# Hymba-style encoder layer on one core: when the three lent weight pieces are issued

## The reference, cut to what matters

```python
def hier_moe(h, w_group, b_group, w_expert, b_expert, w_gate, w_up, w_down):
    ...
    # top-1 group of 4, then top-2 of its 8 experts: expert_idx (T, 2), gates (T, 2)
    flat_e = expert_idx.reshape(A)
    order = jnp.argsort(flat_e)
    ...
    xb = h_pad[buf_tok].reshape(n_blocks, MOE_BLOCK, D)
    def expert_block(args):
        x_b, e = args
        hid = jax.nn.silu(x_b @ w_gate[e]) * (x_b @ w_up[e])
        return hid @ w_down[e]
    ...
    y_assign = yb[dest_orig].reshape(T, TOP_K, D)
    return jnp.einsum('tkd,tk->td', y_assign, gates.astype(h.dtype))
```

## Time and profile before

| | |
|---|---|
| median of 3 runs | 865.64 us (865.56 to 866.73) |
| the profiled execution's own time | 866.06 us |
| its span, first to last instruction | 864.2 us |
| granted TensorE clock, mean | 0.994 |
| PE busy | 833.4 us (96%) |
| DVE, ACT, POOL busy | 414.7, 216.0, 139.9 us |
| moved by DMA | 261.94 MB, 303 GB/s over the span |
| DMA, GB/s in the 22 slices (21.6 us each) from 346 us on, without the last two | 317 to 422 |

### The profile page before, as it was taken

How to read it: one execution, slowest core, us unless ns; L and a number is a source line. 1 busy time by engine, 2 the same in 40 slices (tenths; PEclk the granted TensorE clock), 3 DMA queues, 4 the chain that set the end, 5 groups by cost and what they waited for, 6 DMA issues and landing times.

```text
span 864.2 us, 16000 instructions
## 1 busy us (share of the span) xinstructions
PE 833.4 (96%) x5930; PEld 566.9 (66%) x5931; DVE 414.7 (48%) x796; ACT 216.0 (25%) x461; POOL 139.9 (16%) x279
## 2 busy tenths in 40 slices
PE   7999999999999999899999999999999999999995
PEld 5888988777877887765555555555555555555541
DVE  4699999986565532753222222222222222222237
ACT  3423211457875333101111011110111101111013
POOL 3300010000000011112222212222112222122101
PEclk9999999999999999999999999999999999999999
DMA  7353544221254198899999999999999999999998
GB/s 198 79 137 101 185 178 177 59 87 35 76 168 127 69 414 333 317 363 407 418 418 418 375 411 419 414 420 419 419 419 419 422 419 420 420 419 422 419 385 318
DMA packets 81141, 261.94 MB, mean 303 GB/s; under 512 B 19273, under 2 KB 45129, under 8 KB 56522
## 3 DMA queue, kind: packets, MB, share of 16 engines
q1 hardware_dynamic: 63392, 240.92, 71.3%
q0 software_dynamic: 7888, 18.78, 5.6%
q10 hardware_dynamic: 9818, 1.66, 1.0%
HBM read 246.49 MB, written 24.20 MB: 313 GB/s over the span
## 4 chain that ended last, share of the span: by engine, by line
PE 81%; DVE 13%; DMA 2%; issue 2%; ACT 1%; SPq 1%; POOL 0%; POOLq 0%; DVEq 0%; ACTq 0%
PE ps L1468 29%; PE ps L1514 16%; PE ps L1203 9%; PE ps L1339 8%; DVE big L1945 7%; PE ps L1482 3%; PE ps L1408 3%; PE ps L1255 2%; PE ps L1222 2%; DMA big<-results 2%; PE ps L1234 1%; PE ps L1471 1%; PE ps L1162 1%; DVE w_split L1882 1%; DMA results<-big,to_of 1%
## 5 line engine op out<-in xcount | busy, mean ns | idle before, releaser
L1471 PE MATMUL ps<-ring,big 128*64 128x256 f32 x688 | 154.1, 382 | 0.6 <-DMA ring<-in_w_up 0.6
L1468 PE MATMUL ps<-ring,big 128*64 128x256 f32 x672 | 150.4, 382 | 1.6 <-issue 1.6
L1203 PE MATMUL ps<-hT,w_split 128*128 128x256 f32 (+1 forms) x744 | 136.9, 341 | 0.0
L1468 PEld LDWEIGHTS ps<-ring,big 128*64 128x64 f32 x672 | 92.6, 138 | 56.0 <-issue 12.5
L1203 PEld LDWEIGHTS ps<-hT,w_split 128*128 128x128 f32 x744 | 113.5, 190 | 20.5 <-issue 7.0
L1807 ACT ACTIVATE big<-ps 64x256 f32<-64x256 f32 x78 | 29.3, 376 | 389.4 <-PE ps L1471 346.9
L2234 DVE TENSOR_TENSOR big<-ps,big 64x256 f32<-64x256 f32 x78 | 33.2, 426 | 181.5 <-ACT big L1807 170.9
L1471 PE MATMUL ps<-big 128*64 128x256 f32 x544 | 120.2, 379 | 0.0
L1468 PE MATMUL ps<-big 128*64 128x256 f32 x544 | 120.2, 379 | 0.0
L1468 PEld LDWEIGHTS ps<-big 128*64 128x64 f32 x544 | 74.5, 137 | 46.5 <-issue 9.7
L1471 PEld LDWEIGHTS ps<-ring,big 128*64 128x64 f32 x688 | 94.7, 138 | 2.0 <-DMA ring<-in_w_up 1.0
(11 more groups left out here) (294 smaller groups left out, 1196.5 us busy)
## 6 DMA issues: line engine op xcount, KB each, us to landing
ring<-in_w_down SPq DMA_DIRECT2D x44, 1024.0 KB
ring<-in_w_up SPq DMA_DIRECT2D x43, 1024.0 KB, 14.5
ring<-in_w_gate SPq DMA_DIRECT2D x42, 1024.0 KB, 11.2
big<-in_w_gate SPq DMA_DIRECT2D x20, 1024.0 KB, 7.2
big<-in_w_up SPq DMA_DIRECT2D x20, 1024.0 KB
big<-in_w_down SPq DMA_DIRECT2D x20, 1024.0 KB
w_raw<-in_w_in SPq DMA_DIRECT2D x20, 512.0 KB, 3.9
results<-spare POOLq DMA_DIRECT2D x12, 512.0 KB, 3.2
```

Of the source, the lines that this page charges most:

```text
L1203: mm = pe.matmul(ps[:, n % 2, 0:size], w_split[:, sub, hi_w, k, :], hT[:, k // 4, hi_h, k % 4, cols], **flags)
L1468: pe.matmul(ps[0:BLK, 6 * h, 0:FH], xT[:, k, q, :], gate[2][:, k, fs], **flags)
L1471: mm = pe.matmul(ps[BLK:2 * BLK, 6 * h + 1, 0:FH], xT[:, k, q, :], up[2][:, k, fs], **flags)
```

## The change

Lent piece 0 now waits until `pool_passed` is 1, the other two until it is 2 (in place of the first gather's landing). POOL counts `pool_passed` up behind each of the first two gathers.

```diff
@@ -906,8 +906,9 @@
                 _, _, w, ks = pieces[0][b]
                 sp.dma_start(lent[:, b], weights_of(SLOTS, w, ks)).then_inc(lent_in[b // 2], 16)
 
+            sp.wait_ge(pool_passed, 1)
             load_lent(0)
-            sp.wait_ge(xb_in[0], 16)
+            sp.wait_ge(pool_passed, 2)
             load_lent(1)
             load_lent(2)
 
@@ -1087,6 +1088,7 @@
             for q in range(2):
                 pool.wait_ge(idx_ready, q + 1)
                 fetch(q)
+                pool.sem_inc(pool_passed, 1)
             pool.wait_ge(xb_copied, 1)
             pool.wait_ge(idx_ready, 3)
             fetch(0)
```

## The result

| | before | changed |
|---|---|---|
| median | 865.98 us | 869.84 us |
| lowest, highest of 12 | 864.79, 867.85 | 867.21, 870.75 |
| profiled execution, own time and span | 866.06, 864.2 us | 869.46, 867.6 us |

The ratio is 1.0042, with a 95% interval of 1.0035 to 1.0049: 3.0 to 4.2 us slower. The forecast was 867.8 us, with a range to 869.6. The direction was right; the time lies 0.2 us outside the range. Disturbed executions (three of the kernel before at 1001 to 1195 us, two of after_dve at 885 and 950 us) are left out of every median and ratio of this document.

The account below looks back on a forecast made before the run. PE was taken as the bound, busy 833.4 of 864.2 us. Delays of 1.9 + 0.3 = 2.2 us on the profiled 866.06 gave 868.3, less 0.42 for the median: 867.8 us, range 865.4 to 869.6.

Parts of the forecast that it names:

- When the increment fires: POOL's increment behind the first gather comes at 359.6, bounds 359.0 and 361.1, before the descriptors are written at 361.04.
- Who goes first: First gather goes behind piece 0's megabyte already under way, landing 1.9 us late on PE's path; bounds 0 and 2.4 us.
- The rival of shared DMA engines: Gather packets alternate with piece 0's packets, making the gather 0.3 to 1.1 us late; 866.4 us, chance 0.15.
- Pieces 1 and 2: Second gather waits behind them, landing 0.6 us later than a plain shift; 0.3 us on PE, between 0 and 1.0.
- The half clock: Rival: PE's low clock behind L1416 covers L1416 too or lasts into block 0; 1.5 us more, 869.3 us, chance 0.10.
- A delay of PE before 490 reaches the end in full, a delay of the weights costs nothing: Rule for the sum: the transfers' stall from 490 to 495 us makes up late weights, while transfers behind it hang on PE.

Follow-up runs that it names:

- after_dve: Changed kernel with DVE's copy of the second gather's rows moved behind the one-hot matrix and block 0's first hidden half; 869.0 us, ratio 1.0043 to before.
- engine_inc: Changed kernel with each increment attached to a small fill on POOL's engine behind the gather; 865.55 us, ratio 0.9995 to before.
- first_only: Kernel before, with only piece 0 waiting for the first increment; pieces 1 and 2 wait for the first gather's landing; 868.60 us, ratio 1.0032.
- two_ahead: Kernel before, with pieces 0 and 1 following the first increment and piece 2 waiting for the first gather's landing; 871.11 us, ratio 1.0069.
- second_only: Kernel before, with only pieces 1 and 2 waiting for the second increment; piece 0 issued as before; 866.76 us, ratio 1.0013.
- after_again: Changed kernel once more, unchanged, for a second profile and more timed runs; 869.71 us, ratio 1.0047 to before.
- delay_only: Kernel before, with 9 filling products in place of 3 on PE ahead of the wait for the first gather; 865.33 us, ratio 0.9998.
- landed_fill: Kernel before, with pieces 1 and 2 waiting for the second gather's landing and 9 filling products in place of 3 ahead of L1408; 865.56 us, ratio 1.0000.
- after_busy: Changed kernel with 9 filling products in place of 3 on PE ahead of the wait for the first gather; 869.53 us, ratio 1.0050 to before.

## Why the prediction was right or wrong

**When the increment fires** (359.6, "the sequencer gets past a gather in at most 0.7 us"): right. SP's row was at 359.92 - 0.27 = 359.65 on the clock of before, where 359.7 was forecast, and engine_inc shows that the time up to the end of the engine's row is what matters: an increment behind that end takes the whole loss away. By the Trainium skill (PSUM, section on engine and sequencer instructions) too a sequencer's increment waits for dispatch alone; this case agrees.

**Who goes first, 1.9 us**: right, 1.91 us of wait on PE (before 0.2 us on PEld), and 1.9 us in first_only. The rival of shared DMA engines fell here, and comes back in part with two transfers ahead (two_ahead). The Trainium skill's turns (DMA: Bandwidth & Descriptors, section on queues, rings and completion order) fit that if the first turn is a whole transfer's share of an engine. A piece's share is 8 packets of 8 KB, as the prediction counted; if such a packet is one of the page's descriptors, that is less than the 9 to 17 of a turn, and page and trace agree. But in two_ahead some 0.3 MB of the second piece went ahead of the gather too, and what a turn is, no run here settles.

**Pieces 1 and 2, 0.3 us**: this is the step that failed. Its sentence was "waits again, now behind the first part of two megabytes and not their end", with a landing of 374.2 between 373.6 and 375.2. DVE's copy behind it started at 375.86 - 0.27 = 375.6, outside both bounds, because the gather started some 1.1 us later than a plain shift and its packets were then spread between those of the second piece for another 1 us. The price, "between 0 and 1.0 us", was 1.47 us of waits on PE and +1.36 us in second_only. The two places of slack that the step counted, 0.49 us on DVE and about 0.6 of the 0.7 us on PE, were there, but DVE waited 1.93 us longer than before. By these slacks a landing 0.6 us late would have cost nothing; the 0.3 was a value between the bounds and not their outcome. The step also priced only the first of the two turnings at L1482; the second waited 0.36 us.

**The half clock, a rival at 0.10**: much too small a chance. The mechanism was seen in after_again as it was written ("if low clock covers L1416 too, or lasts longer into block 0"), at 0.94 us and not 1.5. Runs at 0.991 or less are far more frequent than before (10 of 18 against 10 of 75), which speaks for it in many executions. The first profile's 3.18 us hold none of it, and the difference of the medians is more, 3.86 us and in after_again 4.38 us. These 0.7 to 1.2 us fit this cause, but only two profiles of the changed kernel show the clock's course, and the intervals of the ratios are nearly as wide, so the share is not settled.

**The 2.0 us between forecast and median**, 867.8 and 869.84: 0.34 us is the kernel before, whose median of 12 runs was 865.98 and not 865.64. Some 1.0 us (3.18 in place of 2.2) is the step of pieces 1 and 2. The other 0.7 us is what the half clock may explain.

**"A delay of PE before 490 reaches the end in full, a delay of the weights costs nothing"**: the first half held for the changed kernel, where the stall at 490 remained; delay_only, 0.92 us late at block 1, is between 1.0 us shorter and 0.7 us longer than before, so it did not hold in full there. The second half may hold only as long as the stall is left; landed_fill suggests it.

## What to carry to other kernels

A semaphore that a sequencer counts up behind a transfer says that the transfer was passed on, not that its descriptors exist: to let a small transfer go first, attach the count to something that the engine does behind it, or wait for the landing. A small transfer that many wait for, and that meets a large one under way, waited here for the rest of it, up to 1.9 us for 1 MB, and a second large one behind it spread its packets further. When a wait grows, follow what stands behind it in the waiting engine's program; the slack to count with is that of the next instruction that another engine needs.

## What the runs showed of the hardware that was not expected

The first gather's 80 packets waited for the 1 MB under way and then moved in 0.9 us when nothing followed (363.8 to 364.6 in the changed kernel); among the packets of a second megabyte they took 2.1 us (two_ahead). The second gather of the changed kernel took 3.1 us so, before 2.1 us.

Around the same 48 matmuls of one column the granted clock was half for 3.4 us (before, behind them), 6.8 us (after_again, from the turning of the rows on), 10.2 us (two_ahead, 364.9 to 375.2, from the wait for the gather on), or not at all (delay_only, landed_fill). So the 48 matmuls are not needed for the fall: in two kernels it came ahead of them. Eighteen filling matmuls ahead of the rows' turning went with a full clock when the first gather was on time, and not when it was late (after_busy). What decides it stays open.
